# Weight panels in two places instead of three, and the ring left to the next stage

## The reference

```
def first_block(x, c, ...):                       # depth 1
    x = x + gate1 * hybrid_mixer(modulate(x), ...)  # attention and gated delta rule
    x = x + gate2 * routed_moe(modulate(x), ...)    # 32 experts, top 4
    return rms_norm(x, final_norm_w)

def routed_moe(h, w_router, b_router, w1, b1, w2, b2):
    # each token goes to 4 of 32 experts
    # expert e: clamped_swiglu(xb @ w1[e] + b1[e]) @ w2[e] + b2[e]
    # w1[e]: 1024 x 2048, w2[e]: 1024 x 1024

def second_block(x, ...):                         # depth 2
    # layer 0: retention mixer (ret_w_in, ret_w_o), then a squared-relu MLP
    # layer 1: neighbourhood attention (nat_w_in, nat_w_o), then an MLP
```

## Time and profile before

| what | value |
|---|---|
| median of three runs | 2615.64 us |
| the profiled execution | 2613.86 us |
| its span in the trace | 2611.9 us |
| TensorE busy | 2425.1 us, 93% of the span |
| VectorE busy | 1218.1 us, 47% |
| ScalarE busy | 491.0 us, 19% |
| moved by DMA | 636.08 MB |
| mean granted TensorE clock | 0.976 |

### The profile page before, as it was taken

How to read it: one execution, slowest core, us unless ns; L and a number is a source line. 1 busy time by engine, 2 the same in 40 slices (tenths; PEclk the granted TensorE clock), 3 DMA queues, 4 the chain that set the end, 5 groups by cost and what they waited for, 6 DMA issues and landing times.

```text
span 2611.9 us, 41457 instructions
## 1 busy us (share of the span) xinstructions
PE 2425.1 (93%) x17092; PEld 1545.8 (59%) x17092; DVE 1218.1 (47%) x2432; ACT 491.0 (19%) x646; POOL 25.8 (1%) x46
## 2 busy tenths in 40 slices
PE   6998999999999999999799999989999999987998
PEld 5887643333332233323276877767888877765997
DVE  2446433222222223222454353538545566776876
ACT  1211110000000000000122313222222213332432
POOL 0000000000000000000000000000000000000000
PEclk8999999999999999999999999999999999998999
DMA  8788899999999999999721212212322223231652
GB/s 344 297 315 329 316 377 421 422 422 422 422 422 422 422 422 422 422 422 422 323 81 65 82 64 81 81 49 97 113 97 96 96 81 103 96 126 65 226 183 74
DMA packets 90616, 636.08 MB, mean 244 GB/s; under 512 B 10128, under 2 KB 10784, under 8 KB 15600
## 3 DMA queue, kind: packets, MB, share of 16 engines
q1 hardware_dynamic: 85904, 616.93, 59.7%
q0 software_dynamic: 4608, 17.66, 2.0%
HBM read 633.50 MB, written 1.05 MB: 243 GB/s over the span
## 4 chain that ended last, share of the span: by engine, by line
PE 64%; DMA 25%; DVE 7%; issue 2%; ACT 1%; SPq 1%; DVEq 0%; ACTq 0%
DMA hid<-in_panels_e 22%; PE bank L203 10%; PE bank L1844 10%; PE bank L1825 9%; PE bank L1712 6%; PE bank L1764 3%; PE bank L1698 3%; PE bank L1319 3%; PE bank L1176 2%; DMA ring<-in_units_a 2%; PE bank L1743 2%; PE bank L1921 1%; PE bank L1903 1%; PE bank L1248 1%; DVE scratch L3124 1%
## 5 line engine op out<-in xcount | busy, mean ns | idle before, releaser
L203 PE MATMUL bank<-hid,scratch 128*32 128x512 f32 x544 | 234.7, 607 | 0.0
L203 PE MATMUL bank<-hT,scratch 128*32 128x512 f32 x544 | 228.6, 594 | 0.0
L203 PE MATMUL bank<-ring,scratch 128*32 128x512 f32 x2048 | 226.4, 594 | 0.0
L203 PEld LDWEIGHTS bank<-ring,scratch 128*32 128x32 f32 x2048 | 63.0, 110 | 149.1 <-issue 146.4
L203 PE MATMUL bank<-diag_gtmp,scratch 128*32 128x512 f32 x752 | 116.1, 593 | 28.1 <-DMA hid<-in_panels_e 28.1
L2610 DVE TENSOR_SCALAR scratch<-bank 128x512 f32<-128x512 f32 x32 | 22.1, 692 | 250.6 <-PE bank L203 250.6
L978 ACT ACTIVATE scratch<-scratch 128x512 f32<-128x512 f32 x32 | 20.1, 630 | 625.3 <-DVE scratch L2606 625.3
L2993 DVE TENSOR_TENSOR w_lo<-ring,w_hi 128x2048 fp32r<-128x2048 f32 x46 | 105.4, 2291 | 67.5 <-ACT w_hi L1066 67.4
L203 PE MATMUL bank<-rows,scratch 128*32 128x512 f32 x752 | 116.2, 594 | 16.0 <-DMA hT<-in_panels_e 16.0
L2606 DVE TENSOR_SCALAR scratch<-bank 128x512 f32<-128x512 f32 x32 | 22.1, 692 | 224.3 <-PE bank L203 224.3
L1825 PE MATMUL bank<-hT_hi,w_hi 128*128 128x512 f32 (+1 forms) x352 | 126.0, 358 | 0.8 <-ACT mtmp L1077 0.8
(11 more groups left out here) (560 smaller groups left out, 4918.8 us busy)
## 6 DMA issues: line engine op xcount, KB each, us to landing
ring<-in_panels_e SPq DMA_DIRECT2D x128, 1024.0 KB, 23.2
ring<-in_units_a SPq DMA_DIRECT2D x88, 1024.0 KB, 7.2
hid<-in_panels_e SPq DMA_DIRECT2D x64, 1024.0 KB, 25.3
hT<-in_panels_e SPq DMA_DIRECT2D x64, 1024.0 KB, 23.7
ring<-in_panels_m SPq DMA_DIRECT2D x64, 1024.0 KB, 5.1
yacc<-in_panels_e SPq DMA_DIRECT2D x32, 1024.0 KB, 23.0
diag_gtmp<-in_panels_e SPq DMA_DIRECT2D x32, 1024.0 KB, 23.4
rows<-in_panels_e SPq DMA_DIRECT2D x32, 1024.0 KB, 21.8
```

The source lines that it names most:

```text
L203: m = self.pe.matmul(b[s:s + STRIP, :], lhs(k)[:, s:s + STRIP], v, start=(first and k == 0), stop=(k == KT - 1))
```

## The change

`wide` loses its third place, the one over `ring`. Panels now go to two places in turn, and `panels_of_two` waits two panels back instead of three, since it takes the number from `len(wide)`. Panel 2 is no longer loaded by `first_panel` but by `panels_of_two` like those behind it. The first four units of retention wait for the end of the first stage's units instead of the end of the last panel; in SP's stream they stand right behind the last panel's loads.

```
         wide = [(halves(yacc[:, 2:4, :].rearrange("p a b -> p (a b)"), diag_gtmp[:, :]), halves(hid)),
-                (halves(gate_row, cst[:, tail:tail + 2048]), halves(hT)), (halves(ring[:, 0]), halves(ring[:, 1]))]
+                (halves(gate_row, cst[:, tail:tail + 2048]), halves(hT))]
...
             first_panel(rows_ready, XT, 1, 0)
             first_panel(tiles_free, 2, 1, 1)
-            first_panel(unit_used, late + 2, 2, 0)
-            first_panel(unit_used, late + 4, 2, 1)
-            loads.n += 3
-            for j in range(3, 6):
+            loads.n += 2
+            for j in range(2, 6):
                 panels_of_two((pe_[j], pe_[6 + j]), loads)
...
-            sp.wait_ge(E["done"], static)
+            sp.wait_ge(unit_used, len(order))
             ret_loads = Count()
```

## The result

The changed kernel is slower: a median of 2628.61 us in five runs (2626.97 to 2630.51) against 2615.64 (2613.2 to 2615.78), a ratio of 1.0052 with a 95% interval of 1.0038 to 1.0067. Forecast were 2626.4 us and 2621 to 2634. The profiled executions are 2626.97 and 2613.86 us, with spans of 2624.9 and 2611.9: 13.0 us to explain, where my sum had 10.7.

The account below looks back on a forecast made before the run. The prediction took the expert stage alone to be limited by its loads, at 422 GB/s. Its terms, 9.94 + 0.8 + 0 + 0 = 10.7 us, on the median of 2615.64 gave 2626.4 us, range 2621 to 2634.

Parts of the forecast that it names:

- Part 1: Expert stage's start: panel 2 isn't loaded ahead, so the load queue is dry one panel's time longer, +9.94 us.
- Part 2: Early expert stage, TensorE still slower: queue dry again at panel 8, +0.8 us; TensorE meets the loads near 518 us.
- Part 3: Steady state of the expert stage: with two places the queue never runs dry and keeps 422 GB/s, cost 0.
- Part 4: Retention's start: its first four units, loaded early behind the last panel, gain 0 and compete with nothing.
- 1 (dry in each turn): Expert stage: the queue runs dry in 15 more turns, 12 us more, 22.7 in sum, 2638.3 us; chance 0.08.
- 2 (short queue faster): Expert stage: a shorter queue moves 428 GB/s, 13.2 us back, 2.5 us faster than before, 2613.1 us; chance 0.04.
- 3 (retention earlier): Retention's start: early units gain up to 4.65 us, so only 6.1 us slower, 2621.7 us; chance 0.04.
- 4 (no cost): Expert stage: TensorE, not the queue, is the limit in some part, so a place less is free, 2615.6 us; chance 0.03.
- 5 (a start for each half panel): Expert stage: 188 half panels each meet an empty queue, about 1.5 us each, 282 us, 2898 us; chance 0.01.

Follow-up runs that it names:

- e7: Changed kernel with only one of retention's first four units issued early, the other three waiting for the last panel's end: 2623.92 us, ratio 1.0034.
- e1: Changed kernel (two places), but retention's first four units wait for the end of the last panel, as before: 2626.66 us, ratio 1.0041.
- e4: Kernel before, plus four 1 MB copies from DRAM to an unread DRAM buffer issued behind the last panel: 2621.96 us, ratio 1.0022.
- e5: Changed kernel run and profiled once more, no edit, compared with the kernel before on the same chip: 2627.43 us, ratio 1.0047.
- e6: Kernel before, with the ring used for panel 2 alone, loaded ahead; panels 3 to 95 go to the other two places: 2621.2 us, ratio 1.0019.
- e8: Kernel before, plus one 1 MB copy from DRAM to an unread DRAM buffer behind the last panel: 2616.14 us, ratio 0.9997.
- e2: Changed kernel with two of retention's first four units early, the other two waiting for the last panel's end: 2622.76 us, ratio 1.0032.

## Why the prediction was right, and where it wasn't

**Part 1 was right.** The queue restarts with one panel more to go, and E - S grows by 9.42 us where I had 9.94. By the means of the three profiles without an idle time of a panel (937.2) and of the other seven (945.4) it is 8.2. What the remaining 0.5 to 1.8 us are isn't settled; the first 20 us behind the restart differ from run to run (357 to 412 GB/s in 362 to 372 us in the three with the panel in time).

**Part 2 was wrong, in two ways.** The 0.8 us don't exist, and I could have seen it ahead. Panel 3 of the kernel before starts at 351.02 and its panel 9 is issued at 411.44, six panels later. That is the same distance, held against the same bound, as for panels 2 and 8 after. So if it was a loss, both kernels had it, and it had no place in a difference. In fact neither had it: the share is 1.02 and 1.05 in the two microseconds from 411 to 413 of the kernel before, and 1.04 in both of the changed one. The sum had taken the mean rate from the restart on, and the engines were behind it: from 351.02 to 411.44 us the kernel before moved 23.5 MB of panels and not 25.2, so four microseconds of work still lay in the queue. The second miss is the moment at which TensorE meets the loads. I had 518 us; it is 442.09, for the first half of panel 10:

```profile
442.09 0.63 PE L203 MATMUL bank<-yacc,scratch 128*32 128x512 f32 x3 [1.28 <-DMA hid<-in_panels_e]
```

I had let a panel land when its bytes would have passed at the mean rate, about 438. They (8.5 panels, 35.7 MB) had passed only at 440, and TensorE started 2 us behind that. As the loads set the end of the stage in either case, this cost nothing in the sum.

**Part 3 was right.** Share 1.01 and 422 GB/s with two places, 15.3 us to landing, TensorE's lateness covered. The 2 us between issue and motion in its margins are shown by no run here; at the restart of the kernel before, the first packets start 1.0 us behind the issue, which only widens the margins. The Trainium skill's rule on the setup cost of a transfer (page "SBUF — State Buffer", section "The DMA setup-cost knee") spoke against the change; the 422 GB/s of a filled queue don't bear it out.

**Part 4 was the step that failed.** Its gain of zero was right, by e7 and by the chain: VectorE takes unit 0 at 1314.49 in its own order. But I wrote that the four units "compete with nothing: they are behind the last panel in the same queue". I had looked only at that queue. The page lists another one, q8, whose packets pass over the same engines, and the row `issue` in the chain is where such a wait shows. Price: 4.15 us in E - N, 2.6 of it waiting and 1.5 the slower products behind it. Only the 2.6 are shown to come from the early units (e1, e4, e5); the slower products stand in e6 and e8 as well, where the packet wasn't late, and whether the change brings them every time stays open. The Trainium skill gives half a hint: in the page "DMA: Bandwidth & Descriptors", section "Issuing engines are not separate DMA queues", transfers that the scalar, sync or gpsimd engine starts run on the same 16 engines and interleave. It says so of these transfers, not of instructions; that the instruction packet shares the engines too is what the trace shows.

The sum, then: 9.42 for 9.94, 0 for 0.8, 4.15 for 0, a start 0.73 earlier and 0.2 at the end that aren't the change's: 13.0 for 10.7. The largest part was foreseen with its mechanism. That the total came out within 2.3 us is in part luck: a loss that doesn't exist (0.8) and a start that happened to be 0.73 earlier offset a part of the 4.15 that was missed.

Of the rivals, 1 (dry in each turn) is out, 2 (short queue faster) is out at 422 GB/s, 3 (retention earlier) too, since E - N never fell under 17.0, and 4 (no cost) and 5 (a start for each half panel) by E - S.

None of the kernels beats the kernel before; e8 equals it.

## What to carry to other kernels

Where a stage begins with the compute engine slower and ends with the loads slower, the number of places is a lead. Here one place less cost about one panel's time once, not once a turn; loading the same panel ahead without keeping the place (e6) moved the idle time to later and left most of it. When you take a difference, hold both kernels against the same bound. And before you put loads early over the end of a loop, ask who was waiting for them and what else the engines carry at that moment: one unit early was harmless, four made TensorE wait 2.6 us longer, and neither gained anything.

## What the runs showed of the hardware that I had not expected

The wait at the exit of the expert loop goes with a packet of 0.02 MB of the instruction queue q8, which passes over the DMA engines: in ten profiles TensorE resumes 1.74 to 1.78 us behind its end. Where the DMA engines are idle or, in e2, a third busy, the packet starts 0.6 us ahead of the last product's end, and even so the gap is 2.07 to 2.50 us, longer where the packet takes longer (0.95 to 1.36 us). With retention's four units on the engines the gap is 2.6 to 2.9 us longer than before (changed kernel, e5), with four copies behind the last panel 3.9 us (e4). Behind the loop, TensorE's program branches over a block for further experts that isn't run here; whether it is this jump that asks for the packet was not tried. The Trainium skill's page "Advanced Engine Details and Errata", section "ISA Cache", speaks of lines of 16 KB, 256 instructions, of which there are only two; no run here counted the lines.

The eight products behind the gap ran in 3.86 to 3.88 us where the gap was 2.07 to 2.21 us (four profiles), and in 5.37 to 6.60 where it was 2.33 to 5.94 (six profiles), with the granted clock at 0.50, its lower level, in 1301 to 1304 us of the changed kernel. That the slower products come with the gap's length is only what these ten rows have in common; it wasn't tried by itself.
